# First layer's input projection in 256-column weight blocks, with the tokens in two halves of 264 and the activations split once

## The reference, cut to what matters

```python
hn = rms_norm(h, mix_norm_g[l])                     # 528 x 1024
proj = jnp.einsum('bld,dp->blp', hn, w_in[l])       # 1024 x 3072 weights
q, k, v, cx, cb, cc = jnp.split(proj, splits, axis=-1)   # six parts of 512 columns
```

## Time and profile before

| what | value |
|---|---|
| median of 3 runs | 2510.73 us |
| the profiled execution, its own time | 2512.24 us |
| span in its trace | 2510.4 us |
| mean granted TensorE clock | 0.967 of full speed |
| TensorE busy (matmul) | 2295.5 us, 91% |
| VectorE busy | 1801.9 us, 72% |
| ScalarE busy | 1427.8 us, 57% |
| GpSimd busy | 285.8 us, 11% |

### The profile page before, as it was taken

How to read it: one execution, slowest core, us unless ns; L and a number is a source line. 1 busy time by engine, 2 the same in 40 slices (tenths; PEclk the granted TensorE clock), 3 DMA queues, 4 the chain that set the end, 5 groups by cost and what they waited for, 6 DMA issues and landing times. The chain is left out here.

```text
span 2510.4 us, 29988 instructions
## 1 busy us (share of the span) xinstructions
PE 2295.5 (91%) x10510; PEld 1587.1 (63%) x10510; DVE 1801.9 (72%) x2298; ACT 1427.8 (57%) x1796; POOL 285.8 (11%) x148
## 2 busy tenths in 40 slices
PE   5998987699999999999999999589998878889989
PEld 3666665456555555555556555367777667777767
DVE  3444754778888888888898888666664665785564
ACT  3344434567777777677777777355554344665543
POOL 0003501310111111111111110000000000030000
PEclk9999988899999999999999999889998989999999
DMA  3113004389999999999999999512222001121200
GB/s 122 67 67 118 1 34 146 114 316 378 370 371 379 376 372 380 374 365 374 380 377 375 372 373 374 201 68 101 101 101 101 1 1 47 44 96 67 101 1 34
DMA packets 156516, 504.73 MB, mean 201 GB/s; under 512 B 12672, under 2 KB 16416, under 8 KB 156432
## 3 DMA queue, kind: packets, MB, share of 16 engines
q1 hardware_dynamic: 152848, 494.98, 52.5%
q0 software_dynamic: 3584, 8.66, 1.5%
HBM read 492.85 MB, written 10.75 MB: 201 GB/s over the span
## 5 line engine op out<-in xcount | busy, mean ns | idle before, releaser
L1352 DVE TENSOR_TENSOR pieces_low<-pieces,pieces_high 128x2048 fp32r<-128x2048 f32 x384 | 873.7, 2290 | 125.5 <-ACT pieces_high L1308 122.5
L1308 ACT ACTIVATE pieces_high<-pieces 128x2048 fp32r<-128x2048 f32 x384 | 733.1, 1917 | 259.9 <-PE ps L1239 259.7
L1239 PE MATMUL ps<-pieces_high,ex_x 128*66 128x512 f32 x2048 | 567.9, 394 | 5.1 <-DVE ex_hidden L1362 3.0
L1239 PEld LDWEIGHTS ps<-pieces_high,ex_x 128*66 128x66 f32 x2048 | 277.7, 137 | 193.6 <-issue 5.8
L533 PE MATMUL ps<-in_a,in_w 128*128 128x512 f32 (+1 forms) x1656 | 389.4, 395 | 10.6 <-DVE in_a L572 10.5
L533 PEld LDWEIGHTS ps<-in_a,in_w 128*128 128x128 f32 (+1 forms) x1656 | 309.2, 188 | 87.5 <-DVE in_a L572 15.5
L572 DVE TENSOR_TENSOR in_w<-ring,in_w 128x512 fp32r<-128x512 f32 (+3 forms) x220 | 150.1, 683 | 245.9 <-ACT in_w L566 245.3
L1239 PE MATMUL ps<-pieces_low,ex_x 128*66 128x512 f32 x1024 | 320.1, 394 | 0.0
L1239 PE MATMUL ps<-pieces_high,ex_h 128*66 128x512 f32 x1024 | 288.8, 394 | 11.0 <-DVE pieces_low L1352 9.2
L566 ACT ACTIVATE in_w<-ring 128x512 fp32r<-128x512 f32 (+3 forms) x220 | 131.8, 601 | 259.3 <-PE ps L533 247.8
L1239 PEld LDWEIGHTS ps<-pieces_high,ex_h 128*66 128x66 f32 x1024 | 136.8, 136 | 109.1 <-DVE pieces_low L1352 20.0
(11 more groups left out here) (377 smaller groups left out, 2452.4 us busy)
## 6 DMA issues: line engine op xcount, KB each, us to landing
pieces<-in_w_gate SPq DMA_DIRECT2D x128, 1024.0 KB, 7.3
pieces<-in_w_up SPq DMA_DIRECT2D x128, 1024.0 KB, 7.5
pieces<-in_w_down SPq DMA_DIRECT2D x128, 1024.0 KB, 8.7
ring<-in_a_w_in SPq DMA_DIRECT2D x12, 2048.0 KB, 7.7
ring<-in_w_in SPq DMA_DIRECT2D x6, 2048.0 KB, 7.7
ring<-in_mem_w_kv SPq DMA_DIRECT2D x4, 2048.0 KB, 8.1
ring<-in_b_w_in SPq DMA_DIRECT2D x4, 2048.0 KB, 7.8
ring<-in_a_w_out SPq DMA_DIRECT2D x2, 3072.0 KB, 13.6
```

Source lines behind the costliest of these rows:

```text
L1239: ins = pe.matmul(ps[0:CAP, banks + c, :], parts[a][:, k0 + k, :], w[b][:, k, c * 512:(c + 1) * 512], start=start and k == 0 and a == b == ...
L1308: nc.scalar.activation(m.high[:, n % NSPLIT, :], m.pieces[:, n % NPIECE, :], ACT.Copy).then_inc(high_done, 1)
L1352: nc.vector.tensor_tensor(m.low_part[:, n % NSPLIT, :], m.pieces[:, n % NPIECE, :], m.high[:, n % NSPLIT, :].bitcast(F32), ALU.subtract).t ...
```

## The change

w_in is cut into twelve blocks of 256 columns, one job each, so the stage has 96 steps of half the weight columns. A new class, `PairGemm`, gives each unit a pair of PSUM banks: a features unit holds its 528 tokens as two halves of 264, one in each bank; a tokens unit holds two token tiles of 256 columns each (the fifth tile, of 16 tokens, is alone in its unit). All products are of the three-part kind, and the plain float32 rest, its ScalarE copy and its transposes are gone. There are three pairs (banks 0 to 5). A features step is 2 units x 3 products x 2 halves = 12 matmuls of 264 columns; a v step is 5 token tiles x 3 products = 15 matmuls of 256 columns. Job 0 splits the activations, all 528 tokens in each of its eight steps, into an area that is kept (`hn1_split`); the other jobs split weights only. One eviction copies both banks of a unit in one ScalarE instruction. The rotation of tile n is placed 2 or 5 steps after its job's end (`turn_at`), VectorE's part three steps after that. The kept area lies where the expert pieces land, so the first three pieces are issued at the beginning of the attention stage instead of the end of this one.

```diff
+    def place_splits(self, slots):
+        tokens = max(self.tokens(job) for job in self.jobs)
+        self.w_split = [self.m.at(f"{self.name}_w{i}", [P, 2, 512], at, F32R) for i, at in enumerate(slots)]
+        self.a_split = [self.m.at(f"{self.name}_a{i}", [P, 2, tokens], at + 4096, F32R)
+                        for i, at in enumerate(slots)]
...
-        return 512 if job.get("rest") or "split" in job else job["act"].shape[2]
+        return 512 if "split" in job else job["act"].shape[2]
...
+    def split_of(self, s):
+        j, k = self.steps[s]
+        for key in ("split", "keep"):
+            if key in self.jobs[j]:
+                return self.jobs[j][key][:, k]
+        return self.a_split[s % self.ns]
+    def multiply(self, pe, unit, w, a, first, last):
+        job, u = self.jobs[unit.job], unit.u
+        cols = self.m.blocks[self.first + unit.job][2]
+        for i, (x, y) in enumerate(((0, 0), (0, 1), (1, 0))):
+            if job["kind"] == "features":
+                lhs, rhs = w[:, x, u * P:min((u + 1) * P, cols)], a[:, y, 0:self.tokens(job)]
+            else:
+                t0, rows = job["tiles"][u]
+                lhs, rhs = a[:, x, t0:t0 + rows], w[:, y, 0:cols]
+            ins = pe.matmul(self.psum(unit), lhs, rhs, start=(first and i == 0), stop=(last and i == 2))
         return ins
...
-    def rest(self, pe, j):
-        job, w = self.jobs[j], self.m.block_view(self.first + j)
-        act, k_tiles = job["act"], self.m.blocks[self.first + j][1]
-        n_units = self.main_units(j)
-        if job["kind"] == "tokens":
-            unit = self.units[self.first_unit[j] + n_units]
-            self.wait_bank(pe, unit)
-            self.float_products(pe, self.psum(unit), lambda k: act[:, k, 512:], lambda k: w[:, k, :],
-                                k_tiles).then_inc(self.ready, 1)
-            return
-        if j:
-            before = self.units[self.first_unit[j] - 1]
-            pe.wait_ge(self.out[before.engine], before.count)
-        self.float_products(pe, self.m.ps[0:META, self.banks, :], lambda k: act[:, k, 512:],
-                            lambda k: w[:, k, :], k_tiles).then_inc(self.rest_ready, 1)
-    def turn_rest(self, pe, n):
-        pe.wait_ge(self.rest_copied, n + 1)
-        for u in range(4):
-            pe.transpose(self.rest_psum(u), self.rest_tokens[:, u * P:(u + 1) * P],
-                         self.m.ident[0:META, 0:META])
     def products(self, pe, after=None):
...
-                if k == 1 and job.get("rest"):
-                    self.rest(pe, j)
-                if s - self.ns - 2 in self.rests:
-                    self.turn_rest(pe, self.rests.index(s - self.ns - 2))
...
+        weights = (self.m.block_view(self.first + j)[:, k, :], self.w_split[s % self.ns][:, :, 0:cols])
         if "split" in self.jobs[j]:
-            return ((self.m.block_view(self.first + j)[:, k, :], self.w_split[s % self.ns][:, :, 0:cols]),)
-        act = self.jobs[j]["act"]
+            return (weights,)
         tokens = self.tokens(self.jobs[j])
-        return ((self.m.block_view(self.first + j)[:, k, :], self.w_split[s % self.ns][:, :, 0:cols]),
-                (act[:, k, 0:tokens], self.a_split[s % self.ns][:, :, 0:tokens]))
...
-                    if s - self.ns - 1 in self.rests:
-                        n = self.rests.index(s - self.ns - 1)
-                        engine.wait_ge(self.rest_ready, n + 1)
-                        self.m.nc.scalar.activation(self.rest_tokens[:], self.m.ps[0:META, self.banks, :],
-                                                    ACT.Copy).then_inc(self.rest_copied, 1)
...
+class PairGemm(SplitGemm):
+    def place_splits(self, slots):
+        self.w_split = [self.m.at(f"{self.name}_w{i}", [P, 2, 256], at, F32R) for i, at in enumerate(slots)]
+    @staticmethod
+    def tokens(job):
+        return L1
+    def main_units(self, j):
+        return 2 if self.jobs[j]["kind"] == "features" else -(-len(TILES1) // 2)
+    def psum(self, unit):
+        pair = self.m.ps[:, 2 * unit.bank:2 * unit.bank + 2, :]
+        if self.jobs[unit.job]["kind"] == "features":
+            return pair[:, :, 0:HALF1]
+        tiles = TILES1[2 * unit.u:2 * unit.u + 2]
+        return pair[0:tiles[0][1], 0:len(tiles), 0:256]
+    def multiply(self, pe, unit, w, a, first, last):
+        psum, u = self.psum(unit), unit.u
+        for i, (x, y) in enumerate(((0, 0), (0, 1), (1, 0))):
+            for b in range(psum.shape[1]):
+                if self.jobs[unit.job]["kind"] == "features":
+                    lhs, rhs = w[:, x, u * P:(u + 1) * P], a[:, y, b * HALF1:(b + 1) * HALF1]
+                else:
+                    t0, rows = TILES1[2 * u + b]
+                    lhs, rhs = a[:, x, t0:t0 + rows], w[:, y, :]
+                ins = pe.matmul(psum[:, b, :], lhs, rhs, start=(first and i == 0), stop=(last and i == 2))
+        return ins
...
-def projection_stage(m, hn, qk, v, raw, turns, rot_work, slot):
+def projection_stage(m, hn, qk, v, raw, turns, rot_work, kept, slots):
     nc, ps = m.nc, m.ps
     halved = lambda t: t.rearrange("p (a b) -> p a b", a=2)
     scale = 64.0 ** -0.5
-    def take_features(to, scale=1.0):
-        def take(step, u, psum):
-            nc.scalar.activation(to(u)[:, 512:], g.rest_psum(u), ACT.Copy, scale=scale)
-            return nc.scalar.activation(to(u)[:, 0:512], psum, ACT.Copy, scale=scale)
-        return take
-    def take_v(step, u, psum):
-        return nc.scalar.activation(v[0:TILES1[u][1], u, :], psum, ACT.Copy)
-    takes = [("features", take_features(lambda u: qk[:, u, :], scale)),
-             ("features", take_features(lambda u: qk[:, 4 + u, :])), ("tokens", take_v)] + [
-        ("features", take_features(lambda u, i=i: raw[:, 4 * i + u, :])) for i in range(3)]
-    jobs = [dict(kind=kind, act=hn, tiles=TILES1, engine="act", take=take, rest=True, early=True)
-            for kind, take in takes]
-    g = SplitGemm(m, "in1", jobs, m.gaps + [slot], banks=5,
-                  rest_tokens=m.at("in1_rest", [META, 512], slot + 8192))
+    def take_features(to, n0, scale=1.0):
+        return lambda step, u, psum: nc.scalar.activation(halved(to[:, n0 + u, :]), psum, ACT.Copy, scale=scale)
+    def take_v(c):
+        def f(step, u, psum):
+            to = v[0:psum.shape[0], 2 * u:2 * u + psum.shape[1], 256 * c:256 * (c + 1)]
+            return nc.scalar.activation(to, psum, ACT.Copy)
+        return f
+    takes = [("features", take_features(qk, 2 * i, scale if i < 2 else 1.0)) for i in range(4)]
+    takes += [("tokens", take_v(c)) for c in range(2)]
+    takes += [("features", take_features(raw, 2 * i)) for i in range(6)]
+    jobs = [dict(kind=kind, act=hn, engine="act", take=take, early=True) for kind, take in takes]
+    for j, job in enumerate(jobs):
+        job["split" if j else "keep"] = kept
+    g = PairGemm(m, "in1", jobs, slots, banks=3)
     rotated = m.sem("in1_rotated")
     rot_taken = m.sem("in1_rot_taken")
+    turn_at = [g.units[n].place + 1 + 3 * (n % 2) for n in range(8)]
...
             g.send(sp)
-            m.send_experts(sp, 3)
...
-            g.products(pe, {KD + 1 + 2 * n: [lambda n=n: rotate(n)] for n in range(8)})
+            g.products(pe, {turn_at[n]: [lambda n=n: rotate(n)] for n in range(8)})
...
-            g.split("dve", dve, {KD + 4 + 2 * n: [lambda n=n: turn(n)] for n in range(8)})
+            g.split("dve", dve, {turn_at[n] + 3: [lambda n=n: turn(n)] for n in range(8)})
...
 def diff_attention_stage(m, qk, v, raw, mixed, at):
...
+        @block.sync
+        def _(sp):
+            m.send_experts(sp, 3)
...
-        columns(dram["w_in"][0], [512] * 6)
+        columns(dram["w_in"][0], [256] * 12)
...
-        projection_stage(m, hn, qk, v, raw, turns, rot_work, m.arena + work + 8 * L1)
+        kept = m.at("hn1_split", [P, KD, 2, L1], m.low_ring, F32R)
+        projection_stage(m, hn, qk, v, raw, turns, rot_work, kept, m.gaps + [m.arena + work + 8 * L1])
```

More of the change, by code:

```diff
@@ L393, in __init__ @@
         self.first, self.ns = m.taken, len(slots)
-        tokens = max(self.tokens(job) for job in jobs)
-        self.w_split = [m.at(f"{name}_w{i}", [P, 2, 512], at, F32R) for i, at in enumerate(slots)]
-        self.a_split = [m.at(f"{name}_a{i}", [P, 2, tokens], at + 4096, F32R) for i, at in enumerate(slots)]
+        self.place_splits(slots)
         self.high = m.sem(f"{name}_high")
@@ L401, in __init__ @@
         self.out = {"act": m.sem(f"{name}_act_took"), "dve": m.sem(f"{name}_dve_took")}
-        self.rest_tokens = rest_tokens
-        if rest_tokens is not None:
-            self.rest_ready, self.rest_copied = m.sem(f"{name}_rest_ready"), m.sem(f"{name}_rest_copied")
-        self.rests = []
         self.steps, self.units, self.first_unit = [], [], []
@@ L416, in __init__ @@
             ring += n_units
-            if job.get("rest") and job["kind"] == "tokens":
-                new.append(Unit(j, n_units, job["engine"], banks))
-                n_ready += 1
```

(29 more changed lines are left out.)

8 lines of the change are left out of this document (2 added, 6 removed).

## The result

The changed kernel takes 2471.12 us (median of four runs, 2467.97 to 2473.53) against 2510.16 us for the kernel before (2509.26 to 2511.52, four executions now): 39.0 us less, a ratio of 0.9843 with a 95% interval of 0.9826 to 0.9860. The forecast was 29.5 us less, 2481.2, in a range from 2475.5. The direction was right, and so was the account of the projection stage up to the pace of its products.

A forecast was written before the change was run, and what follows sets the result against it. TensorE was taken to bound the projection, falling from 187.5 to 158.4 us: 29.1 us less, plus 0.2 at the start and 0.2 at the end, 29.5 in all. Median forecast 2481.2 us, range 2475.5 to 2491.

The forecast's parts named there:

- What bounds the stage: Input projection: TensorE busy 187.49 of 187.6 us, so work it no longer issues there comes off the span.
- The parts removed: Projection, off TensorE: six rests 41.8 us, five groups of transposes 1.8 us, eight edges 1.9 us.
- The products: Projection: 960 of 264 columns at 123.3 ns and 240 of 256 at 120.0, together 147.2 us, 16.2 more than now.
- The constant over the streaming time: Projection products: 14.2, 13.6, 13.5 ns at 512, 384, 320 columns; unmeasured below; spread plus or minus 3 ns, 3.6 us.
- Edges: Projection: extra time of a run of products between other work, 0.24 us each; 9 runs instead of 17, 2.2 us.
- Rival C: Projection: short float32r products run at plain float32's pace, 463 ns each, kernel slower at 2560 or 2887; chance 4%.
- Attention taken over unchanged: Attention: only the moved expert DMAs considered, costed at nothing, upper bound 1 us.
- Later stages: After attention: no term in the sum; a shift of later clock drops by a few us counted as spread.
- Start, end, DMA: Projection's start and end: 0.2 us less each; DMA blocks of 1 MB: nothing, upper bound 4.3 us.
- A: Projection: weight loads put a floor of 123 to 147 ns under short products; kernel 2496 half way, 2510 at full; 8%.
- B: Projection: refills by ScalarE and VectorE come late at job ends and rotations, costing TensorE 10 us, kernel 2491; chance 10%.
- D: Projection: the change does not do what it says, the rest survives; 2481 becomes 2523; chance under 1%.

The follow-up runs named there:

- keep_only: Kernel before with only the once-split, kept activations and the expert pieces issued in attention: 2506.25 us, ratio to before 0.9983.
- split_each: Changed kernel, but every job splits the activations again: 2477.17 us, ratio to before 0.9867.
- norest: Kernel before without the last 16 tokens in the projection (their columns set to zero), so no rest: 2458.28 us, ratio to before 0.9805.
- bridge_before: Kernel before with four unused float32 products of 256 columns at the start of attention: 2501.52 us, ratio to before 0.9967.
- halves_outer: Changed kernel with the two halves as outer loop, so a bank gets three products in a row: 2475.78 us, ratio to before 0.9863.
- before_again: Kernel before, unchanged, measured once more: 2508.21 us, ratio 1.0003.
- delay_before: Kernel before with two unused VectorE memsets at the first norm, making everything behind about 1.7 us later: 2510.93 us, ratio to before 1.0013.
- exp_moved: Kernel before with only the three expert pieces issued in attention instead of at the projection's end: 2507.67 us, ratio to before 1.0000.
- after_again: Changed kernel, unchanged, measured once more: 2474.88 us against 2508.71 for the kernel before, ratio 0.9860.
- delay_after: Changed kernel with two unused VectorE memsets at the first norm, a delay of 1.7 us: 2472.51 us, ratio to before 0.9867.
- longer_gap_after: Changed kernel with one more small GpSimd memset, lengthening TensorE's idle time ahead of attention to 3.24 us: 2476.90 us, ratio to before 0.9872.
- exp_late: Changed kernel with the three expert pieces issued in the router stage instead of attention: 2474.10 us, ratio to before 0.9859.

## Why the prediction was wrong, by its steps

*What bounds the stage: right.* TensorE is busy for the whole of it before and after, and the two kernels that change only its helpers' work (`keep_only`, `split_each`) leave it at 187.2 and 154.9 us.

*The parts removed: right.* 45.5 us were summed for rests, transposes and edges; `norest` measured 46.1.

*The products: the direction right, the size off.* The step "264 columns come to 123.3 ns and 256 to 120.0" gave 147.2 us for them; at 121.4 and 119.1 ns they are 145.1. The constant over the streaming time was not constant below 320 columns: 11.4 and 12.4 ns instead of 13.5. Edges (56.16 to 60.73 is 4.57 us for 36, against 4.37, so 0.20 instead of 0.24), rotations (0.69 us each time, where half had been 0.80) and the clock at the start (2.7 instead of 3.1 us) give 1.2 us more. Together 3.3 of the 3.6 us between 158.4 and 154.8. That is about as much as the spread the forecast allowed for its constant, and would have left the kernel inside the range. Why the constant is smaller there is open; the loop order explains 0.7 of the 1.9 ns at most. (Rival C's 231 ns for plain float32 at 264 columns was read too high, too: the first of those eight records is followed after 285 ns, the others after 222.5. It does not change that rival's case.)

*Attention taken over unchanged: wrong.* This is the step that failed. The forecast named "a shift of later clock drops by a few us" as spread around its time and gave it no price from rows; for attention itself it allowed only for the moved DMAs ("nothing, upper bound 1 us"). In the first pair of profiles attention is 5.5 us shorter. But attention has two lengths. In the 17 profiles of this study it is 98.5 to 99.6 us in eleven and 104.4 to 106.9 in six. All six have a drop to half clock at most 1.5 us from its start and at least one more of 3.4 us, over 45 us before its end; the eleven have neither, or the first alone. The row to read was there: 228.07, 5.43 us for 16 records at 264 columns, where they take 4.01 us at full clock in the changed kernel. `bridge_before` shows that the waits of attention turn this into 6 us, and that it belongs to the kernel before, not to the change. The same mark is in every profile: in the first 50.4 us of attention GpSimd waits five times for TensorE in all six long ones (2.8 us, and 4.4 or 4.5 in `halves_outer` and `split_each`), and never in the eleven short ones. Whether these waits are what makes the lag grow, or only go with it, no run separates. The kernel before and its like had the long form in four of five profiles (`before_again`, `delay_before`, `exp_moved`; `keep_only` is the fifth). The changed kernel and its like, without filling, had it in two of seven. With 5.5 us between the two forms, that difference in frequency would be worth some 3 us on average, an estimate from few profiles. What the nine profiles with an early drop do show is that its place sorts them: where it began between 0.7 us before and 1.2 us after attention's first product, attention was long; where it began 1.3 or 1.4 us after it, the lag of some 0.5 us was gone within 10 us. Why the drop falls there or stays away, and more often in one kernel, is open: delay, moved DMAs and the length of the idle time were tried, and none settles it.

*Later stages: costed at nothing, 2.6 us in the first pair of profiles.* Their 2171.3 to 2180.2 us over all profiles are spread, not a gain; in `after_again`, with 2180.2, they are longer than in the first profile of the kernel before. So part of the first measurement's 39.0 us is luck, and the second's 33.8 is nearly the 29.1 + 0.4 of the forecast plus the projection's 3.6.

*Start, end, DMA: right in size.* The idle time ahead of attention is 0.2 us shorter; the start is 0.6 us earlier in the first profile, but without the added delay or filling starts vary from 35.6 to 38.0 us between profiles. Blocks of 1 MB delayed nothing.

*The rivals.* A (a floor above 123 ns) fell: the pace is 121.4 ns, although the records of the weight loads now have no pause. C (plain float32 pace) fell by the same number. B fell: TensorE is never idle in the stage, and with the old splitting load in `split_each` it still takes 154.9 us. D did not occur. None of the rivals, and nothing in the range, was a mechanism that makes the kernel faster than forecast.

## What to carry to other kernels

Removing TensorE work from a stage that it fills is worth what the rows say: the parts added up to within 2.5% of the stage in three kernels (before, `norest`, after). Price each idle time of TensorE by what its clock does behind it, in the next stage: four unused products between two stages gave the kernel before 7.4 us for one line, a fifth of what this rewrite of a stage gave. In a stage whose engines wait for each other, look for where the lag grows, not only for where the clock is low. And where repeated executions spread by 10 us, a difference of a few us between two profiles needs a second profile of each; a profile of the fastest or slowest execution does not stand for the median.

## What the runs showed of the hardware

Products of float32r at 264 and 256 columns follow each other at 121.4 and 119.1 ns, each with its own weight load. The records of the loads cover 152.5 of the stage's 154.7 us, and yet the time over one column per cycle at 2.4 GHz is 11.4 and 12.4 ns here, less than the 13.5 to 14.2 of the wider products.

TensorE's clock fell to half for 3.4 or 6.8 us at or within 1.5 us of the beginning of attention in nine of 17 profiles. In three of them (`delay_after`, `longer_gap_after`, `exp_late`) it stayed alone, and attention took 99.4 to 99.6 us against 99.3 without it. In the other six attention took 5 us or more longer, with 4.5 to 5.8 us of lag already there at reductions 21 and 22, before the drop that comes 51 to 52 us in. TensorE loses half of the time that it spends at half clock (2.7 us in the 5.7 us at the start of the projection), so at most 1.7 us in a drop of 3.4; the other 2.8 of the 4.5 us of the kernel before arose at full clock, in the waits between the engines.
